# One float32 transformer kernel: unread TensorE products at more stage boundaries, a triangular inverse on 64-wide squares, and two other orders of attention tiles

## The reference

```python
def first_block(x, mem, ...):
    h = rmsnorm(x, g_mix)
    dq, dk, dv, dz, db, da, cq, ckv, kix, wix = split(h @ w_in)
    # gated delta rule, 4 heads of 128; q, k, v after a depthwise convolution
    a_mat = where(strict, beta * (k @ k.T) * decay, 0) + eye      # lower triangular
    u, w  = triangular_solve(a_mat, [v * beta, k * beta * exp(g_cum)])
    for each chunk:                                              # state carried along
        v_new = u - w @ state
        o     = q_dec @ state + where(incl, q @ k.T * decay, 0) @ v_new
        state = state * last + k_dec.T @ v_new
    # sparse attention, 8 heads: the 256 best keys by an indexer, latents of 128 as keys and values
    p     = softmax(where(chosen, q_abs @ c_kv.T / 8 + bias, -1e30))
    o_lat = p @ c_kv
    x = x + concat(rmsnorm(o_dn) * silu(dz), o_lat @ w_uv) @ w_out
    x = x + cross_attention(rmsnorm(x), rmsnorm(mem)) @ w_xo
    hf = rmsnorm(x, g_ffn)
    x = x + (silu(hf @ w_gate) * (hf @ w_up)) @ w_down           # width 2816
    return rmsnorm(x, g_final)

def second_block(x, c, ...):                                     # two layers
    h = rms_norm(x) * (1 + scale) + shift
    y_fox = causal attention, 8 heads of 64, with a forget bias       * silu(gate)
    y_mla = latent attention, 8 heads, 64 + 32 rotary, causal by 64   * silu(gate)
    x = x + gate * (concat(y_fox, y_mla) @ w_out)
    # at the end: rms_norm(x, final_g)
```

## Time and profile before

| | |
|---|---|
| time, three runs | median 3579.76 us (3577.94 to 3579.96) |
| profiled execution | 3583.08 us, its span 3581.3 us, mean granted clock of PE 0.974 |
| PE busy | 3344.4 us (93%) |
| DVE, ACT, POOL busy | 50%, 34%, 30% |
| HBM | 159.92 MB read, 16.87 MB written |

### The profile page before, as it was taken

One profiled execution on the slowest core, in us unless ns is written; L12 is line 12 of the kernel. 1 busy time (PEld: TensorE's weight loads), 2 busy tenths in 40 slices (PEclk: granted clock), 3 DMA queues, 4 the chain that ended last, 5 costly groups with the idle time before them and its releaser, 6 DMA issues. The chain is left out here.

```text
span 3581.3 us, 46879 instructions
## 1 busy us (share of the span) xinstructions
PE 3344.4 (93%) x18302; PEld 2630.0 (73%) x18302; DVE 1789.8 (50%) x3377; ACT 1205.6 (34%) x2253; POOL 1082.3 (30%) x603
## 2 busy tenths in 40 slices
PE   7799998899989899999999989998898999998988
PEld 5477675599878777888888867776666677775667
DVE  3887888555464426544544570335444502345443
ACT  2474566444122311000000130335453212344540
POOL 3133001254354335534534333220112333201112
PEclk9999999899999999999999999999999999999999
DMA  3011000001121113221322113110102211101011
GB/s 125 24 45 38 24 3 1 8 1 54 53 65 54 43 52 126 89 87 59 105 70 66 58 36 106 48 36 13 25 1 83 83 52 44 54 13 18 7 71 71
DMA packets 234300, 179.90 MB, mean 50 GB/s; under 512 B 42944, under 2 KB 219248, under 8 KB 233216
## 3 DMA queue, kind: packets, MB, share of 16 engines
q1 hardware_dynamic: 231376, 176.56, 16.1%
q10 hardware_dynamic: 2736, 0.78, 0.1%
HBM read 159.92 MB, written 16.87 MB: 49 GB/s over the span
## 5 line engine op out<-in xcount | busy, mean ns | idle before, releaser
L1097 DVE SCALAR_TENSOR_TENSOR y_T<-y_T 128x1024 f32<-128x1024 f32 x48 | 137.4, 2914 | 0.1
L876 ACT ACTIVATE I-13465a_hi<-I-13464act_f 128x512 fp32r<-128x512 f32 x22 | 13.5, 633 | 336.8 <-DVE I-13464act_f L885 336.8
L909 DVE TENSOR_TENSOR x_T<-x_T,I-13471p_d 128x512 f32<-128x512 f32 x88 | 60.3, 687 | 126.2 <-PE I-13471p_d L841 126.2
L283 PE MATMUL I-13469p_g<-hf_hi,I-13445w_hi 128*128 128x512 f32 x352 | 108.8, 390 | 3.0 <-POOL hf_lo L518 3.0
L283 PE MATMUL I-13470p_u<-hf_hi,I-13446w_hi 128*128 128x512 f32 x352 | 108.5, 389 | 2.3 <-POOL I-13448w_lo L269 2.3
L285 PE MATMUL I-13469p_g<-hf_lo,I-13445w_hi 128*128 128x512 f32 x352 | 108.4, 389 | 0.0
L287 PE MATMUL I-13469p_g<-hf_hi,I-13447w_lo 128*128 128x512 f32 x352 | 108.4, 389 | 0.0
L287 PE MATMUL I-13470p_u<-hf_hi,I-13448w_lo 128*128 128x512 f32 x352 | 108.4, 389 | 0.0
L285 PE MATMUL I-13470p_u<-hf_lo,I-13446w_hi 128*128 128x512 f32 x352 | 108.4, 389 | 0.0
L1692 DVE TENSOR_TENSOR I-22523S<-I-22523S,c_causal 128x256 f32<-128x256 f32 x32 | 13.8, 431 | 185.1 <-PE I-22523S L1617 185.1
L885 DVE TENSOR_TENSOR I-13464act_f<-I-13463act_g,I-13470p_u 128x512 f32<-128x512 f32 x44 | 28.3, 684 | 155.0 <-PE I-13470p_u L287 155.0
(11 more groups left out here) (1422 smaller groups left out, 10154.6 us busy)
## 6 DMA issues: line engine op xcount, KB each, us to landing
y_T<-in_w_ada SPq DMA_DIRECT2D x48, 512.0 KB, 3.6
saved_x<-x_T SPq DMA_DIRECT2D x3, 4096.0 KB, 13.7
I-13443w_raw<-in_w_gate SPq DMA_DIRECT2D x22, 512.0 KB, 4.6
I-13444w_raw<-in_w_up SPq DMA_DIRECT2D x22, 512.0 KB, 4.2
x_T<-saved_x SPq DMA_DIRECT2D x2, 4096.0 KB, 14.1
I-13457d_raw<-in_w_down SPq DMA_DIRECT2D x11, 512.0 KB, 5.0
I-13458d_raw<-in_w_down SPq DMA_DIRECT2D x11, 512.0 KB, 4.7
I-913w_raw<-in_w_in SPq DMA_DIRECT2D x8, 512.0 KB, 3.8
```

Source lines behind the costliest of these rows:

```text
L283: nc.tensor.matmul(out[h], w_hi[:, k, :], hi(k, h), start=(k == 0), stop=False)
L876: nc.scalar.activation(a_hi[s][:, cols], act_f[:, cols], ACT.Copy).then_inc(a_rounded, 1)
L909: nc.vector.tensor_tensor(x_n, x_n, p_d[n % 2][:, h, :], ALU.add).then_inc(d_added[n % 2], 1)
L1097: self.nc.vector.scalar_tensor_tensor(out=self.raw[s], in0=self.raw[s], scalar=1.0, in1=self.c_row, op0=ALU.mult, op1=ALU.mult, accum_out= ...
```

## The change

It has four parts.

1. Unread products. A new helper `run_on` issues n fp32 products of the 128x128 identity with itself. They stand at the begin of `project_stage` (10), at the end of `latents_stage` (24), at the end of `fox_stage` (5), at the begin (12) and end (5) of `mla_stage`, in `delta_stage` at the begin (18), behind the first sums (8), twice in iteration -1 (8 and 3) and at the end (6), and at the begin of `delta_project_stage` (5). `keep_running` gets longer: `Normed.pe` 3 and 5, the ends of `project_stage` and `delta_project_stage` 18, the end of `ffn_stage` 42.
2. Squares. In `delta_stage` levels 1 to 5 of the inverse work on the two 64x64 diagonal squares of each head alone: T, N, Y and `c_T` are [128, heads, 64], the upper square on partitions 0 to 63, the lower on 64 to 127, and each product becomes two, one on a square each. The turns at these levels are ordinary products with a piece of the identity. Level 6 joins the squares into `whole_N`, whose other corners POOL has set to 0 at the start. `a_T` has two buffers. There is one more table (`c_eye`), and two are smaller.
3. Orders. `sparse_stage` takes the tiles of a head as 7, 1, 5, 3, 6, 0, 4, 2 (its copies out of `aux` then go to every other tile); `mla_stage` takes the tiles of a pair from 7 down to 0, and its gating of the output takes the halves in the other order.
4. In `sparse_stage` the operation L2712 goes; the half of a grid step that stood in L2714 becomes a bias of ACT's second exponential, from a constant that POOL sets once.

```diff
+def run_on(nc, const, n, out):
+    for _ in range(n):
+        nc.tensor.matmul(out, const["c_ident"][:, :], const["c_ident"][:, :], start=True, stop=True)
...
-        keep_running(self.nc, 2, unread, self.ident, self.src[:, 0, 0:BANK])
+        keep_running(self.nc, 3, unread, self.ident, self.src[:, 0, 0:BANK])
         self.ir.pe_spread(pe)
-        keep_running(self.nc, 4, unread, self.ident, self.src[:, 0, 0:BANK])
+        keep_running(self.nc, 5, unread, self.ident, self.src[:, 0, 0:BANK])
...
+                run_on(nc, const, 10, acc[1][:, 0, 0:P])
                 for j in range(KD):
...
-                keep_running(nc, 12, acc[0][:, 0, :], hi[:, 0, 0:P], hi[:, 0, 0:BANK])
+                keep_running(nc, 18, acc[0][:, 0, :], hi[:, 0, 0:P], hi[:, 0, 0:BANK])
...
-                keep_running(nc, 20, p_u[:, 0, :], hi[:, 0, 0:P], hi[:, 0, 0:BANK])
+                keep_running(nc, 42, p_u[:, 0, :], hi[:, 0, 0:P], hi[:, 0, 0:BANK])
...
+    def tile(self, u):
+        return NT - 1 - u % NT if self.falling else u % NT
...
+        behind_whole = t == (NT // 2 - 1 if self.falling else 0)
+        wait(pe, scores_read, 2 * u if t >= NT // 2 or behind_whole else 2 * (u - 1))
...
+                run_on(nc, const, 12, ph.S[:, 3, 0:P])
                 def project(m):
...
                 last.then_inc(returned, 1)
+                run_on(nc, const, 24, norm_sums[:, BANK - P:])
...
-    ORDER = list(range(NT))[::-1]
+    ORDER = [7, 1, 5, 3, 6, 0, 4, 2]
...
-                    nc.scalar.activation(rest[:, 0:w], rest[:, 0:w], ACT.Exp).then_inc(exp_done, 1)
+                    nc.scalar.activation(rest[:, 0:w], rest[:, 0:w], ACT.Exp, bias=half_grid[:, 0:1]).then_inc(exp_done, 1)
...
-                    v.tensor_scalar(least[:, one], least[:, one], GRID_ROUND, None, ALU.add).then_inc(least_shifted, 1)
-                    dve.wait_ge(least_shifted, u + 1)
-                    v.tensor_scalar(neg[:, one], least[:, one], GRID_ROUND, GRID / 2, ALU.subtract, ALU.add).then_inc(bias_set, 1)
+                    v.tensor_scalar(neg[:, one], least[:, one], GRID_ROUND, GRID_ROUND, ALU.add, ALU.subtract).then_inc(bias_set, 1)
...
-                    nc.gpsimd.tensor_tensor(c_T[level - 1][:, :, :], a_T[:, :, :], tiled(low_t[:, level, :], H), ALU.mult).then_inc(c_ready, 1)
+                    nc.gpsimd.tensor_tensor(c_T[level - 1][:, :, :], a_T[n % 2][:, :, 0:CHUNK], tiled(low_t[:, level, :], H), ALU.mult).then_inc(c_ready, 1)
...
-                            last = mm(p_Y[g][:, h, :], c_T[level - 1][:, h, :], t_of(n, h), start=True, stop=True)
+                            if level < STEPS:
+                                for q in SQUARES:
+                                    last = mm(p_Y[g][q, h % 2, :], c_T[level - 1][q, h, :], T[s][q, h, :], start=True, stop=True)
+                            else:
+                                last = mm(p_Y[g][LOWER, h % 2, :], a_T[s][UPPER, h, CHUNK:], T[s][UPPER, h, :], start=True, stop=True)
...
-                                last = turn(p_TN[g][:, 1, h % 2, :], t_of(n, h), ident)
+                                for q in SQUARES:
+                                    dst = p_N[g][q, h % 2, :] if level < STEPS else p_whole[g][q, h % 2, q]
+                                    last = mm(dst, T[s][q, h, :], ident[q, q], start=True, stop=True)
...
-                                last = mm(p_TN[g][:, 0, h % 2, :], n_of(n, h), Y[:, h, :], start=True, stop=True)
+                                for q in SQUARES:
+                                    last = mm(p_T[g][q, h % 2, :], N[s][q, h, :], Y[q, h, :], start=True, stop=True)
...
-                                last = mm(p_TN[g][:, 1, h % 2, :], Y[:, h, :], n_of(n, h), start=True, stop=True)
+                                last = mm(p_whole[g][UPPER, h % 2, LOWER], Y[LOWER, h, :], whole_N[s][LOWER, h, LOWER], start=True, stop=True)
...
+                run_on(nc, const, 18, unread)
+                pe.wait_ge(table_in, 80)
...
+                run_on(nc, const, 8, unread)
                 pe.wait_ge(cols_exp, 3)
+                pe.wait_ge(corner_set, 2)
...
+                    if c < 0:
+                        run_on(nc, const, 8, unread)
...
+                    if c < 0:
+                        run_on(nc, const, 3, unread)
...
+                run_on(nc, const, 6, p_Y[0][:, 0:2, :].rearrange("p a n -> p (a n)"))
```

More of the change, by code:

```diff
@@ L105, in shape_constants @@
         low[:, level] = same & (r[:, None] % (2 * s) >= s) & (r[None, :] % (2 * s) < s)
-    out["c_low0"] = low[:, 0].copy()
-    out["c_low_t"] = np.ascontiguousarray(low.transpose(2, 1, 0))
+    squares = lambda m: np.concatenate([m[:CHUNK, ..., :CHUNK], m[CHUNK:, ..., CHUNK:]])
+    out["c_low0"] = squares(low[:, 0])
+    out["c_low_t"] = squares(low[:, 0:LEVELS - 1].transpose(2, 1, 0))
+    out["c_eye"] = squares(np.eye(P, dtype=f))
     out["c_strict_t"] = (r[:, None] < r[None, :]).astype(f)
@@ L1642, in pe_values @@
     def pe_values(self, pe, u):
-        t, before = u % NT, self.turns_before(u)
-        if t % 4 == 0:
+        t, before = self.tile(u), self.turns_before(u)
+        if u % 4 == 0:
             wait(pe, self.y_ready, u // 4)
@@ L1678, in dve_max @@
     def dve_max(self, dve, u):
-        w, out, s = (u % NT + 1) * P, self.scores_of(u), u % 2
+        w, out, s = (self.tile(u) + 1) * P, self.scores_of(u), u % 2
         dve.wait_ge(self.scores_ready, u + 1)
@@ L1899, in _ @@
                 ph.pe_values(pe, PAIRS * NT - 1)
+                run_on(nc, const, 5, ph.S[:, 3, 0:P])
             @block.scalar
@@ L2651, in aux_copy @@
                     else:
-                        d, h = slice(k // 2 * DH, (k // 2 + 1) * DH), 1 - k % 2
-                        ins = copy(out[d, i, h * BANK:(h + 1) * BANK], aux[d, :])
+                        d, odd = slice(k // 2 * DH, (k // 2 + 1) * DH), 1 - k % 2
+                        every_other = out[d, i, :].rearrange("d (a b n) -> d a b n", b=2, n=P)[:, :, odd, :]
+                        ins = copy(every_other, aux[d, :].rearrange("d (a n) -> d a n", n=P))
                     ins.then_inc(aux_out, 1)
@@ L2992, in _ @@
                 nc.gpsimd.memset(state[:, :, :], 0.0).then_inc(state_set, 1)
-                pool.wait_ge(table_in, 64)
+                for t in whole_N:
+                    nc.gpsimd.memset(t[:, :, :], 0.0).then_inc(corner_set, 1)
+                pool.wait_ge(table_in, 80)
                 spread_gates(0)
                 for c in range(-1, NT):
-                    for level in range(3, LEVELS):
+                    for level in range(3, STEPS):
                         off_diagonal(c, level)
@@ L3188, in copy_below @@
                         act.wait_ge(y_done[g], STEPS * n + level)
-                        copy(halves(Y, g), halves(p_Y[g], g)).then_inc(y_copied[g], 1)
+                        if level < STEPS:
+                            copy(halves(Y, g), p_Y[g][:, 0:H // 2, :]).then_inc(y_copied[g], 1)
+                        else:
+                            copy(Y[LOWER, GROUPS[g], :], p_Y[g][LOWER, 0:H // 2, :], -1.0).then_inc(y_copied[g], 1)
                         if level > 1:
                             act.wait_ge(t_turned[g], TURNS * n + level - 1)
-                            copy(TN[n % 2][g][:, 1, :, :], p_TN[g][:, 1, :, :]).then_inc(n_copied[g], 1)
+                            if level < STEPS:
+                                ins = copy(halves(N[n % 2], g), p_N[g])
+                            else:
+                                wait(act, v_done, n - 1)
+                                wait(act, w_done, n - 1)
+                                ins = copy(whole_N[n % 2][LOWER, GROUPS[g], LOWER], p_whole[g][LOWER, :, LOWER])
+                            ins.then_inc(n_copied[g], 1)
                 def exponentials(n):
@@ L3206, in copy_matrix @@
                     act.wait_ge(a_turned, n + 1)
-                    wait(act, c_ready, STEPS * n)
-                    copy(a_T[:, :, :], F[2][:, :, :]).then_inc(a_copied, 1)
+                    wait(act, c_ready, IN_SQUARES * (n - 1))
+                    for g in range(2):
+                        wait(act, y_done[g], STEPS * (n - 1))
+                    copy(a_T[n % 2][UPPER, :, :], F[2][UPPER, :, :]).then_inc(a_copied, 1)
+                    copy(a_T[n % 2][LOWER, :, 0:CHUNK], F[2][LOWER, :, LOWER]).then_inc(a_copied, 1)
                 def copy_keys(n):
@@ L3278, in first_inverse @@
                         wait(dve, t_done[g], STEPS * (n - 1))
[L3279 to L3283 removed]
+                    for q in SQUARES:
+                        v.tensor_tensor(T[n % 2][q, :, :], a_mat[q, :, q], tiled(low0[q, :], H), ALU.mult).then_inc(t_masked, 1)
+                    dve.wait_ge(t_masked, 2 * (n + 1))
+                    v.tensor_tensor(T[n % 2][:, :, :], tiled(eye[:, :], H), T[n % 2][:, :, :], ALU.subtract).then_inc(t_set, 1)
                 def weigh_queries(n):
@@ L3322, in subtract @@
```

(14 more changed lines are left out.)

97 lines of the change are left out of this document (52 added, 45 removed).

## The result

The changed kernel takes a median of 3545.16 us (3541.75 to 3548.61, four runs) beside 3579.86 of the kernel before on the same chip: a ratio of 0.9903, 95% interval 0.9886 to 0.992. It is 1% faster, and inside the range, but by 34.7 us, not by 72: less than half of the forecast. A second comparison gave 0.9908 (0.9893 to 0.9923). The profiled execution took 3548.56 us with a span of 3546.7, that is 34.6 shorter than the span before.

The account below looks back on a forecast made before the run. TensorE, busy 93% of 3581.3 us, was taken as the bound. Delta rule -37, sparse -11, mla -10, boundaries -14 make -72: 3583.1 - 72 - 3.3 = 3508 us; range 3482 to 3556, the forecast's own 3488 to 3530.

Parts of the forecast that it names:

- rival 1: Delta rule: the two squares don't run at once, a couple costs two records; 3550 or 3570 us; chance 0.20.
- 136 x 0.065 = 8.8 us, 4.1 less than now: Delta rule's inverse, per chunk: 120 couples and 16 single records at 65 ns each, against 12.9 us before.
- -23: Delta rule, chunks 1 to 6: each 3.9 us shorter after 0.2 of waits, 23 us in all.
- 8.5: Delta stage's setup and end: 5.0 us less in the setup and 3.5 less in chunk 7.
- No more than 2.1 a head can go: Sparse attention: a head of 30.27 us has PE busy 28.12, so at most 8 x 2.1 = 17 us.
- 1.4 a head: Sparse attention: gain taken for alternating large and small tiles, -11 us in all, ends 0 and -17.
- -10: Latent attention (mla): falling tile order cuts PE's waits for DVE's L1708, -5 us a layer; ends 0 and -16.
- The products and the spread behind them gain: End of ffn_stage: 42 unread products keep the clock full, so gates' sums take 3.6 us, products and spread gain 1.
- -1.4: Project stages' starts: 10 unread products let eight passes at 0.43 us become 0.227; -1.4 us at each of three.
- -4.0: Unread products at the end of ffn_stage, through faster sums, products and spread in the gates: 4.0 us less.
- Or if unread products end later than what they waited beside: Sign that the prediction is wrong: unread products at the boundaries overrun the wait meant to cover them.
- Rival 5: Stage boundaries: the edits do nothing to the clock, boundaries 0 to +10 us, total 3522 to 3532; chance 0.06.

Follow-up runs that it names:

- e_only_unread: The kernel before with all the added unread products but the delta stage's: 0.05 to 0.24% slower than the kernel before, 2 to 9 us.
- e_no_unread: The changed kernel without any of the added unread products, the delta stage's included; squares and orders as changed: 3543.11 us.
- e_after_again: The changed kernel run once more, unaltered, for a second comparison on the same chip; a second comparison of the changed kernel gave 0.9908 to the kernel before.
- e_falling_sparse: The changed kernel with the sparse attention's tiles from 7 down to 0 again, L2712 still removed: 3554.7 us, 0.993; the stage takes 258.24 us.
- e_micro: The changed kernel plus a stage ahead of the final one issuing only unread products of mixed shapes: 3734.53 us, 191 us of it the extra stage.

## Why the prediction was half right

Of the forecast 72 us, 37 are missing in the profiles: 13 in the delta rule, 6 in the sparse attention, 20 in all other stages, less 1.5 that mla gave more. The time lies in the range only because the range was widened to reach the rivals; it is outside the forecast's own 3488 to 3530. The number nearest to it is rival 1's 3550, and its mechanism (squares that don't run at once) did not hold: that is luck.

- **Squares: right in the mechanism, the size off.** The step that failed is "136 x 0.065 = 8.8 us, 4.1 less than now": it has a price per couple and none for changing from squares to full products, eleven times a chunk. The couple is cheaper than taken (58.3 ns for 65): 256 x 0.0292 = 7.5 us. Eleven changes at 0.34 add 3.7: 11.2. Against 12.9, and the 0.6 that the steps from full to transposed or 128-wide inverse products already cost before (11 x 0.053, the table), this gives 2.3 saved a chunk; the windows give 2.34. Six middle chunks: -14, not -23. Chunk 0 gave 3.8 for 5.4 (20.37 to 16.60 between its first sums and the next chunk's); setup and end 5.8 for 8.5. I had bounded the couple from both sides, and not asked whether a mix of shapes costs what its parts cost: no row before has a 64x64 record beside a full one.
- **Sparse: the bound was read over too short a stretch.** "No more than 2.1 a head can go" came from one head. The pattern of waits repeats over two heads, not one: PE is busy 58.30 of 60.46 us in two (above), so 1.1 a head was all there was; the head that I had picked held both waits. The order took nearly all of it (58.37 of 58.38). "1.4 a head" was above the ceiling. Then the first head gave some back, which rows of the timeline show:

```profile
374.89 1.11 PE L2621 MATMUL I-2926PT<-c_ident,I-2912probs 128*128 128x128 f32 x4 [3.12 <-DVE I-2912probs L2739]
375.79 1.06 PE L2621 MATMUL I-2927PT<-c_ident,I-2912probs 128*128 128x128 f32 x4
376.65 3.19 PE L2603 MATMUL I-2924S<-x_T,I-2907q_abs 128*128 128x512 f32 x4
```

  A short tile behind the first long one leaves nothing to do for 3.12 us, and the scores behind it run at half clock (3.19 us where the same records take 1.88 in a later head).
- **mla: right**, -11.5 for -10, by the wait that was named.
- **Boundaries: the step failed.** "The products and the spread behind them gain", -14 in sum; shown is +2 to +9 (e_only_unread). The forecast took a full clock for time. Where the full clock went is read at four places. (1) project_stage: the first passes run at full clock behind the unread ones, and PE then waits for POOL's weights, whose rounding starts 8.1 us into the stage as before, released by DVE's yx_lo:

```profile
1212.29 2.47 PE L362 MATMUL I-13177acc<-c_ident 128*128 128x128 f32 x20 [1.49 <-PEq L194]
...
1220.34 3.94 POOL L267 TENSOR_TENSOR I-13166w_hi<-I-13165w_raw,c_ones 128x1024 fp32r<-128x1024 f32 x1 [7.96 <-DVE yx_lo L747]
...
1226.79 0.73 PE L285 MATMUL I-13177acc<-yx_hi,I-13166w_hi 128*128 128x512 f32 x2 [0.90 <-POOL I-13167w_lo L271]
```

  The forecast has -1.4 here; from barrier to barrier this stage takes 96.95 to 97.15 us in all thirteen profiles, with the added products and without. So here the gain is shown to be nothing, and why. (2) ffn_stage to gates_stage: the wait of 5.98 us became 1.10, and the clock fell all the same, during the sums of one column (rows above); the second stretch of unread products then runs at that level too. In e_only_unread it did not fall there:

```profile
2080.05 3.70 PE L384 MATMUL I-15496token_sums<-c_ones,y_T 128*128 128x1 f32 x32 [1.10 <-PEq L192]
```

  gates_stage takes 126.2 us in that profile, 126.7 to 128.7 in the other eight with the added products, and 129.4 to 129.6 in the four without: a part of the -4.0 came, though ffn_stage scatters too much to show what 22 products more cost at its end. (3) delta_project_stage: the faster products before it end sooner, PE waits longer for DVE (3.09 us for 1.59), the clock falls, and 32 spread records take 6.5 us that took 3.6 before (from 899.95 to 903.54); first the row of before, then rows of after:

```profile
899.95 2.05 PE L409 MATMUL I-9894m_tps<-c_ident,I-9925inv_tok 128*128 128x128 f32 x16 [1.59 <-DVE I-9925inv_tok L400]
```

```profile
872.98 3.78 PE L416 MATMUL I-10220m_tps<-c_ident,I-10251inv_tok 128*128 128x128 f32 x16 [3.09 <-DVE I-10251inv_tok L407]
876.55 3.19 PE L416 MATMUL I-10215acc<-c_ident,I-10251inv_tok 128*128 128x128 f32 x16
879.50 0.71 PE L3488 MATMUL I-10214acc<-y_hi,I-10202w_hi 128*128 128x512 f32 x2
```

  They take 4.9 to 6.5 us in seven of the eight profiles that have the changed kernel's full set of these products, and 3.6 in the eighth, in the four without and in e_only_unread. (4) The begin of delta_stage: the 36 records (18 unread products) run at half clock for a part of their time (granted clock 0.70) and end after the tables' landing, so that the first sums start 5.76 us into the stage; after:

```profile
667.31 5.88 PE L362 MATMUL I-6721F<-c_ident 128*128 128x128 f32 x36 [1.99 <-PEq L194]
673.03 0.31 PE L3187 MATMUL I-6724p_Y<-decay,I-6715upper 128*128 128x32 f32 x2
```

  and in e_no_unread, whose stage begins at 665.42, 3.93 us into it:

```profile
669.35 0.64 PE L3181 MATMUL I-6698p_Y<-decay,I-6689upper 128*128 128x32 f32 x2 [5.87 <-DMA I-6693eye<-in_c_eye]
```

  "Or if unread products end later than what they waited beside" was named as what would make the forecast wrong; here it did. (In e_after_again and e_falling_sparse the 36 records had the full clock and took 4.26 us; there the last table landed later, and the first sums came 5.4 and 5.6 us into the stage, behind a wait for it.) The setup then wins part of it back (between the first sums of iteration -1 and those of chunk 0: 9.97 us with the unread products, 11.02 and 11.48 without, 14.62 before). In all, chunk 0's first sums come 17.97 us into the stage, and 17.10 and 17.76 without. (3) as it is in after and (4) are not in e_only_unread, so they don't explain its loss: which places make up the +2 to +9 stays open. Rival 5 says this of the boundaries, "0 to +10", though not by its reason that the clock would not rise.
- **The bound.** The 93% busy PE gave the direction; but a busy PE was also what hid the cost of shapes: it is counted as busy time.

## What to carry to other kernels

Price a mix of tile shapes by the mix: measure a round of small and large products, not a run of each, and count how often the order changes between them; but count also what the large ones in between cover. Before a bound is read from one unit of a loop, look how long its pattern of waits is. To keep the clock up brings no time where another engine's work ends last, as POOL's in project_stage: ask which engine is next, and compare a kernel with nothing but those products added.

## What was not expected of the hardware

- A change between 64x64 square products and full 128x128 ones costs 0.34 us there and back; in the same rounds products on row halves give 0.39 and on column halves 0.35 (rounds of 2.18 and 2.11 us; 56.2 and 54.6 ns a record inside long runs). These figures are those of one stage and one order of operands.
- Two square records on different corners start 6 to 7 ns apart and the next pair 52 ns later: 29.2 ns a record. The Trainium skill (TensorE: Matmul & The Clock Gate, section "Wait — 56ns, not 53.3ns?") gives a floor of about 62 ns for a matmul when the hardware decode is off; whether it is off here no run shows. As a price per record the runs disagree with it, and the measurement decides; a couple of records has 58.3.
- The granted clock fell to half where PE had idled for 1.10 us only and then worked at sums of one column (0.66 in the window from 2058). So it did in seven of the nine profiles with that wait; in e_only_unread and e_micro the same sums ran at 1.00, in 3.70 us. What decides it is not shown.
- The same kernel's profiled executions had 137 and 109 us at the lower clock level and took 3548.56 and 3536.58 us; which stages differ changes from run to run.
